# Two scratch tensors in HBM laid out by block instead of packed by group, in a decoder step's expert layer

## The reference

```python
v1, i1 = lax.top_k(s1, PEER_TOPK)          # 16 best of 128 keys, two key sets, 8 heads
v2, i2 = lax.top_k(s2, PEER_TOPK)
cand = (v1[..., :, None] + v2[..., None, :]).reshape(...)
sc, ci = lax.top_k(cand, PEER_TOPK)
eid = (jnp.take_along_axis(i1, ci // PEER_TOPK, -1) * N_KEYS + jnp.take_along_axis(i2, ci % PEER_TOPK, -1))
gate = jax.nn.softmax(sc, -1)
hid = jax.nn.gelu(jnp.einsum('td,thkd->thk', xt, expert_u[eid]))
return jnp.einsum('thk,thkd->td', (gate * hid), expert_v[eid])
```

## Time and profile before

| | before |
|---|---|
| median of 3 runs | 2101.7 us (2099.17 to 2104.75) |
| profiled execution, own time | 2104.75 us |
| its span | 2103.0 us |
| TensorE busy | 2018.1 us, 96% |
| VectorE busy | 1619.7 us, 77% |
| ScalarE busy | 794.4 us, 38% |
| GpSimd busy | 542.5 us, 26% |
| mean granted TensorE clock | 0.979 of full speed |
| moved by DMA | 483.75 MB, mean 230 GB/s |

### The profile page before, as it was taken

How to read it: one execution, slowest core, us unless ns; L and a number is a source line. 1 busy time by engine, 2 the same in 40 slices (tenths; PEclk the granted TensorE clock), 3 DMA queues, 4 the chain that set the end, 5 groups by cost and what they waited for, 6 DMA issues and landing times.

```text
span 2103.0 us, 33945 instructions
## 1 busy us (share of the span) xinstructions
PE 2018.1 (96%) x12943; PEld 1851.9 (88%) x12943; DVE 1619.7 (77%) x3030; ACT 794.4 (38%) x1311; POOL 542.5 (26%) x334
## 2 busy tenths in 40 slices
PE   8999889889999899999999999999989999999998
PEld 8998879778866899999999999999978888888886
DVE  6735766565254325999999799999969999999997
ACT  4335453342241322232244344444434333333332
POOL 0000020000000000212111045555537656666530
PEclk9999989989999999999999999999999999999999
DMA  5224210061451402677676579999999999999992
GB/s 172 81 89 129 81 52 1 22 225 41 166 197 62 160 1 89 222 279 247 225 245 237 184 238 334 330 333 333 334 375 396 411 412 411 411 411 411 407 353 93
DMA packets 205520, 483.75 MB, mean 230 GB/s; under 512 B 11983, under 2 KB 104655, under 8 KB 205286
## 3 DMA queue, kind: packets, MB, share of 16 engines
q1 hardware_dynamic: 159334, 314.56, 41.3%
q0 software_dynamic: 46080, 167.79, 21.7%
HBM read 423.29 MB, written 58.36 MB: 229 GB/s over the span
## 4 chain that ended last, share of the span: by engine, by line
PE 58%; DMA 1%; SPq 1%; ACT 0%; DVE 0%; issue 0%; POOL 0%; DVEq 0%
PE ps L3001 24%; PE ps L2609 8%; PE ps L2605 8%; PE ps L2604 8%; PE ps L2595 5%; PE ps L2633 4%; DMA outputs<-peer_v,kept 1%; SPq L2563 0%; SPq L2586 0%; DMA experts<-peer_u 0%; ACT scores L2690 0%; DMA hidden<-kept 0%; PE ps L3027 0%; PE ps L3032 0%; ACT kept L2679 0%
## 5 line engine op out<-in xcount | busy, mean ns | idle before, releaser
L3001 PE MATMUL ps<-v_high_low,gated_high_low 128*128 128x512 f32 x2304 | 526.1, 390 | 8.2 <-ACT gated_high_low L3069 7.4
L3001 PEld LDWEIGHTS ps<-v_high_low,gated_high_low 128*128 128x128 f32 x2304 | 434.0, 189 | 100.1 <-ACT v_high_low L3067 7.7
L2604 PE MATMUL ps<-x_high_low,u_high_low 128*128 128x384 f32 x1024 | 355.6, 347 | 0.2 <-ACT u_high_low L2670 0.2
L2605 PE MATMUL ps<-x_high_low,u_high_low 128*128 128x384 f32 x1024 | 345.0, 337 | 0.0
L3093 POOL DMA_INDIRECT outputs<-peer_v,kept x138 | 255.8, 1854 | 155.7 <-DVE kept L3110 121.5
L2721 POOL DMA_INDIRECT scores<-peer_u,kept x64 | 95.1, 1485 | 733.5 <-DVE kept L2841 556.9
L2679 ACT ACTIVATE kept<-ps 128x384 f32<-128x384 f32 x128 | 62.9, 491 | 407.5 <-PE ps L2609 404.3
L2609 PE MATMUL ps<-x_high_low,u_high_low 128*128 128x384 f32 x1024 | 204.7, 341 | 0.0
L2604 PEld LDWEIGHTS ps<-x_high_low,u_high_low 128*128 128x128 f32 x1024 | 192.5, 188 | 0.5 <-ACT u_high_low L2670 0.5
L2605 PEld LDWEIGHTS ps<-x_high_low,u_high_low 128*128 128x128 f32 x1024 | 192.8, 188 | 0.0
L3110 DVE SCALAR_TENSOR_TENSOR kept<-outputs,kept 128x1024 f32<-128x1024 f32 x136 | 174.3, 1281 | 8.9 <-DMA outputs<-peer_v,kept 5.5
(11 more groups left out here) (471 smaller groups left out, 4136.7 us busy)
## 6 DMA issues: line engine op xcount, KB each, us to landing
experts<-peer_u SPq DMA_DIRECT2D x63, 1024.0 KB
raw_v<-peer_v SPq DMA_DIRECT2D x60, 1024.0 KB
hidden<-kept SPq DMA_DIRECT2D x64, 384.0 KB, 3.5
gates<-scores SPq DMA_DIRECT2D x12, 2048.0 KB
first_hidden<-hidden SPq DMA_DIRECT2D x16, 768.0 KB, 10.4
outputs<-gates SPq DMA_DIRECT2D x16, 768.0 KB
outputs<-hidden SPq DMA_DIRECT2D x16, 768.0 KB
first_gates<-gates SPq DMA_DIRECT2D x15, 768.0 KB
```

Source lines behind the costliest of these rows:

```text
L2604: pe.matmul(o, utr[:, b, HI, k], xr[:, HI, k, 0:DN], start=(k == 0), stop=False)
L2605: pe.matmul(o, utr[:, b, HI, k], xr[:, LO, k, 0:DN], start=False, stop=False)
L3001: ins = pe.matmul(bank(c, 2 * t + h), gr[:, slot, x, DN * b + P * t:DN * b + P * t + P], vr[:, slot, y, D * b + 512 * h:D * b + 512 * h + ...
```

## The change

Both helpers go, and every load and store uses the tensors' own shapes. The gates lie in HBM as token group, block, token: a store of gates is one run of 16 KB per partition (128 runs instead of 4096), and a load of one group is 12 runs of 512 bytes per partition (1536 instead of 128). The hidden values lie at a pitch of 544 floats: a store of two blocks is two runs of 1536 bytes per partition, and a load of four blocks four such runs. The bytes, the buffers on the chip, the semaphores and the order of everything stay.

```diff
@@ phase_hidden, SyncE
-                sp.dma_start(hidden_rows(c)[:, bass.ds(q * UG, UG)], hid[:, slot]).then_inc(hid_stored[slot], 16)
+                sp.dma_start(c.hidden_dram[:, bass.ds(q * UG, UG), 0:DN], hid[:, slot]).then_inc(hid_stored[slot], 16)
...
-                sp.dma_start(gates_by_group(c)[:, :, bass.ds(tg, 1)].rearrange("p n g x -> p (n g) x"), gst[slot].rearrange("p (n b) t -> p n (b t)", b=GB)).then_inc(gates_stored[slot], 16)
+                sp.dma_start(c.gates_dram[:, bass.ds(tg, 1)].rearrange("p g k t -> p (g k) t"), gst[slot]).then_inc(gates_stored[slot], 16)
...
-                    sp.dma_start(hid_first, hidden_rows(c)[:, 0:4]).then_inc(c.first_gated, 16)
-                    sp.dma_start(gates_first[:, 0:NTG - 2].rearrange("p g b t -> p (g b t)"),
-                                 gates_by_group(c)[:, 0, 0:NTG - 2].rearrange("p g x -> p (g x)")).then_inc(c.first_gated, 16)
+                    sp.dma_start(hid_first, c.hidden_dram[:, 0:4, 0:DN]).then_inc(c.first_gated, 16)
+                    sp.dma_start(gates_first[:, 0:NTG - 2].rearrange("p g b t -> p g (b t)"),
+                                 c.gates_dram[:, 0:NTG - 2, 0:4].rearrange("p g b t -> p g (b t)")).then_inc(c.first_gated, 16)
@@ phase_combine, SyncE
-                sp.dma_start(gt[slot].rearrange("p g b t -> p (g b t)"),
-                             gates_by_group(c)[:, bass.ds(g, 1)].rearrange("p n g x -> p (n g x)")).then_inc(g_in[slot], 16)
-                sp.dma_start(ht[slot], hidden_rows(c)[:, bass.ds(g * GB, GB)]).then_inc(h_in[slot], 16)
+                sp.dma_start(gt[slot].rearrange("p g b t -> p g (b t)"),
+                             c.gates_dram[:, :, bass.ds(g * GB, GB)].rearrange("p g b t -> p g (b t)")).then_inc(g_in[slot], 16)
+                sp.dma_start(ht[slot], c.hidden_dram[:, bass.ds(g * GB, GB), 0:DN]).then_inc(h_in[slot], 16)
```

More of the change, by code:

```diff
@@ L2462 @@
 DOTS_BY = {4: 0, GT: 16, 0: 32, 1: 46, 2: 59}
[L2465 to L2472, removed]
 def phase_hidden(c):
```

## The result

The changed kernel takes 2118.56 us (median of four runs, 2118.05 to 2120.36) against 2101.99 us (four runs, 2099.17 to 2104.75): a ratio of 1.0081, 95% interval 1.0066 to 1.0095. It is slower by 16.6 us, twice and a half what a measurement can tell. The forecast was 2102.5 us, its range 2096 to 2117.

A forecast was written before the change was run, and what follows sets the result against it. The prediction took TensorE to set the output stage's pace, with DMA full too and 0.41 us spare per group. It summed -1.5 - 1.9 + 4.2 = +0.8 us, giving 2102.5 us, range 2096 to 2117.

The forecast's parts named there:

- dear pieces: Output stage: short-run loads cost 0.78 us per group or more; sign: TensorE's products from 1600 to 2000 us fall 2% or more.
- The lead of the cast at block 112: Output stage: ScalarE's cast of expert rows was to end near zero ahead of TensorE at block 112, instead of 8.6 us.
- Part 1: Search stage: each gate store takes 0.9 us less DMA time, but ten of the 12 save nothing because products cover them.
- Part 2: Behind the gate store of 1519.30: TensorE's wait for the last expert rows goes, -1.5 us (bounds 0 and -1.5).
- Part 3: Behind the gate store of 1548.43: the last hidden store is issued earlier, -1.9 us (bounds 0 and -2.75).
- The rival of 9.7 us: Switch of stages, 1520 to 1580 us: a free SyncE removes all of TensorE's idle time, 2092 us; chance 0.12.
- Part 4, the size: Output-stage loads in shorter runs: +0.57 us of DMA time per group, 0.16 short over 26 groups, +4.2 us.
- my upper bound: Output-stage loads: at most +1.10 us of DMA time per group, 26 x 0.69 = +18 us.
- Part 4, the lead: Output stage: gathers run up to four rows ahead once, 5.1 us, which the expert rows' 5.8 us ahead of TensorE pay.
- Part 5: First gates and hidden values +0.2 us; SyncE standing up to 3.9 us behind each output-stage gate load, costed at nothing.
- The likeliest case: Output-stage loads cost 0.41 to 0.78 us more per group: 2098 to 2108 us; chance 0.40.
- the case of dearer pieces: Output-stage loads cost 0.78 us more per group or above: 2116 us at 1.10, 2111.6 at 0.92; chance 0.35.

The follow-up runs named there:

- e2_hidden_only: Kernel before, with only the hidden values' stores and loads in the tensor's own shape and the gates packed as before: 2103.64 us, ratio 1.0011.
- e4_gate_loads_only: Kernel before, with only the gates' loads as in the changed kernel (1536 runs of 512 bytes), stores still packed: 2116.64 us, ratio 1.0078.
- e6_before_more_bytes: Kernel before, plus one extra load per group from group 2 on, 3 KB per partition in one long run: 2121.83 us, ratio 1.0106.
- e3_gate_stores_only: Kernel before, with only the gates' stores as in the changed kernel (128 runs of 16 KB), loads in the old packed order: 2098.8 us, ratio 0.9993.
- e10_after_ring4: Kernel after, all loads whole, with the gathers held to four rows ahead of VectorE throughout instead of eight from the 21st row: 2117.18 us, ratio 1.0082.
- e5_after_half_hidden: Kernel after, but from group 2 on the hidden load brings two of the four blocks, gate loads unchanged: 2100.54 us, ratio 1.0000.
- e9_half_hidden_ring4: Kernel after, with two of four hidden blocks loaded per group and the gathers held to four rows ahead of VectorE throughout: 2097.78 us, ratio 0.9984.

## Why the prediction was wrong, point by point

**What bounds it.** Right: DMA and TensorE both full in the output stage, with 0.41 us of DMA time to spare per group. All that followed turned on this, and the window after shows what was asked for there: products down by 5.6% (a fall of 2% was named as the sign of dear pieces), DMA share full. The 0.41 is itself a little high: from block 24 to 112 VectorE uses 122 rows, 5.55 a group, which leaves some 0.32 at 411 GB/s. The lead of the cast at block 112 is 2.9 us instead of 8.4, at blocks 16, 20, 48 and 56 it is 0.56 us, none at all.

**Parts 1 to 3, the search stage and the switch: -3.4.** Part 1 (ten stores save nothing) is right. Part 2: TensorE no longer waits for the last expert rows; its window of 1520 to 1540 us is full. Part 3: the store is issued right behind its Gelu. In the profiled pair the way to block 4 is shorter by 3.5 us, as forecast. That closeness is partly luck: over all runs the four with the old stores (before, e2_hidden_only, e4_gate_loads_only, e6_before_more_bytes) average 237.4 us to block 4, the seven with 16 KB stores 235.5. The gain is about 1.9 us by that, with single runs 2 us apart; e3_gate_stores_only has it at 1.5 us by its ratio of 0.9993, with an interval that touches 1. The rival of 9.7 us is out: 53.59 of 60 us are busy instead of 50.34, so 6.4 us stay idle.

**Part 4, the size: the failed step.** I took the row of 326 GB/s for the 512-byte runs, +0.50 us per group, and half way to 383 GB/s for the runs of 1536 bytes, +0.07. Sorting all packets from 1700 to 2000 us by size and fitting the time that each size takes of the 16 engines gives 27.6 ns per run of 512 bytes, 67.7 ns per 1536, about 160 per 4 KB, and 237.9 per 6 KB before. Per engine and group that is 96 x 27.6 - 8 x 237.9 = +0.75 for gates and 32 x 67.7 - 8 x 237.9 = +0.26 for hidden values: **+1.01 us, not +0.57**. As rates, 27.6 ns a run are 297 GB/s and 67.7 ns are 363, not the 326 and 397 that I took. The plain rate agrees: 6.54 MB at 385 GB/s are 16.98 us per group, 1.07 more than 15.91. Both are nearly my upper bound, 1.10, which came from the 293 GB/s and the 351 GB/s rows. I had set the first aside as perhaps not full, and the second as a long stretch; the output stage is itself a long stretch in which nothing is idle, and 351 GB/s was the row with that in common. From block 24 to 112 there are 22 groups: 22 x (1.01 - 0.41) = 13.2 us; measured 13.0. The number in the formula was wrong; that the two agree so closely is partly luck. 1.6 of the 13.0 us are the clock, for which the sum had no term, and some work of these blocks had been done ahead. e10_after_ring4, with the same loads, no fall of the clock and little fetched ahead, lost 16.3 us in the same blocks. The Trainium skill ("DMA: Bandwidth & Descriptors", "Why small descriptors are slow (HBM only)") has some 3 cycles per packet beside one per 32 bytes, from which I had worked out an estimate of +0.40 us. The runs show two and a half times that, so here the measurement decides against the page's figure.

**Part 4, the lead: the second failed step.** I had the gathers run ahead once, by up to four rows, 5.1 us, and let the lead of 5.8 us pay for it. The run-ahead is real and larger, 5.2 rows more than before at block 20, and it came on top of the growing deficit. I had taken three of SyncE's packets to one of the gathers' from a gate store; under the gate loads it was one to one, 559 beside 563, so 0.5 KB of SyncE's bytes against 4 KB. The result: the lead went (5.5 to 0.56 us at block 20) and TensorE lost 9.3 us as well by block 24, 1.7 of them at half the clock. Had I kept the one-time cost in the sum instead of setting it against the lead, my upper bound would have been 18 + 5.1 - 3.4, about 2121 us, and the time inside the range. There is a second lesson in it. Before, the 0.41 us of spare wasn't idle: the share is full all along, and the gathers use part of it to run ahead, 2.8 rows at block 20 and 6.0 at block 104, while the lead of the cast grows. A spare that another queue eats first isn't there for the queue that needs it. In e6_before_more_bytes 26 x 0.54 = 14.0 us were worked out and 21.8 lost behind block 4. The clock is 5.7 of the difference; that the gathers' run-ahead is the rest is argued, since no run holds them back there.

**Part 5, SyncE's standing: right at nothing from block 24 on.** Its size was off: up to 3.9 us expected, 6.1 in the median, up to 12.96 seen. But e5_after_half_hidden keeps it and loses nothing behind block 24, and e6_before_more_bytes loses all without it. Much of the standing takes the place of a wait that was there before. Before, SyncE issued the first expert load of a pair in 0.38 us and then waited until TensorE was done with the blocks of the second. The timeline shows such a pair as one row; the waits have it by name, 54 of them, up to 7.8 us long:

```profile
1628.63 7.33 SPq L2984 DMA_DIRECT2D raw_v<-peer_v  x2
```
```profile
SPq L2984 <- PE ps L3001: 257.3, 54, 7.8
```

From 1600 to 2000 us this wait is 207.1 us before and 7.1 after: SyncE had time to spare, and the standing uses it up.

Its own share between blocks 16 and 24 isn't isolated. A stand of 7.59 and 6.94 us cost at most 0.7 us there (e10_after_ring4), and 5.5 us were lost with none (e6_before_more_bytes). But the kernel after stood 12.96 and 9.85 us, and its expert rows were asked for some 14 us behind TensorE's start of block 14, where it was 1.6 us before; holding the gathers back shortened this too.

**The sum.** -3.4 + 4.2 = +0.8 was forecast; -3.5 + 22.3 is what the profiled pair shows, and 16.6 what the medians show. The likeliest case had no more than 0.78 us per group; the case of dearer pieces, at 1.10, gave 2116 us, near the truth, with a chance of 0.35. Its reason is right for the blocks from 24 on (13.0 us) and has nothing of the 9.3 us before them; that its 18 us come so near the 22.3 of both is luck.

## What to carry to other kernels

- When a stage has DMA and an engine full at the same time, work out the spare per group. Then price a change of run length by the slowest row of a long, full stretch, not by the best short one: here +1.01 us against 0.41 of spare decided everything.
- Shorter runs on the side that is read under load cost more than long runs save on the side that is written under cover. The 31 loads decide; ten of 12 stores are free.
- A queue that may run ahead takes the spare first. Before you let a lead pay for something, ask who else draws on it; and test a suspected stall by keeping it and removing the load elsewhere, since a loss as large came without the longest bar of the timeline (12.96 us).

## What the runs showed of the hardware

- Under full load, in the output stage, a run costs a fixed time beside its bytes: 27.6 ns for 512 bytes, 67.7 for 1536, about 160 for 4096 and 237.9 for 6144 (fits over 300 us, good to about 1 ns). The difference of the first two, 40.1 ns for 1024 bytes, leaves 7.5 ns for a run of no bytes, which is drawn out of the fit and not measured. The long ones lie a little under that line (168 and 248 ns).
- A DMA of 1536 runs makes the next issue on SyncE's queue take 6.1 us in the median; one of 768 runs 0.4 us in the median and up to 4.49, with up to 5.50 at the expert load behind it. Gate stores of 4096 runs cost 10.4 us, stores of 128 runs 0.5. The same 1536 runs cost 4.6 us where the gathers were held back and half the hidden values loaded (e9_half_hidden_ring4). So it isn't a fixed cost per run; a queue of fixed room that has to drain would behave so, which no run shows directly.
- The shares between queues follow packets, not bytes: from 1628 to 1634 us of the kernel after, 559 packets of SyncE's queue with its 512-byte runs passed beside 563 of the gathers, mostly 4 KB each, and took 16.7% of the engines' time against 87.8%. Over the 20 us around it the gathers took 60.6%, against 43.9% before. Beside a gate store in the search stage it was 350 to 136, so the ratio isn't the same everywhere.
- A wait of TensorE can cost more than its length. In e6_before_more_bytes the granted clock fell to half in the course of waits of 3.15 and 2.87 us and stayed there for 6.8 us each: 5.7 us on top. In the kernel after it cost 3.3 us.
